# Modulation product in four column groups, attention steps respread over the units, and the values product behind the next step's scores

## The reference, cut to what matters

```
m = silu(cond) @ w_ada + b_ada            # two conditioning vectors (latent, context), 6 * 2048 columns
h = rmsnorm(x) * (1 + sc1) + sh1          # needs the first 2 * 2048 columns of m
u = h @ w_in                              # GLU input | q | k | v | gate A | gate B
att = softmax with sink over (own keys in a window of +-128, 256 cached keys) @ values
mixed = (sigmoid(gA) * conv(glu) + sigmoid(gB) * (att @ w_attn_out)) @ w_out
x = x + g1 * mixed                        # then a mixture of 16 experts and a last norm
```

## Time and profile before

| | |
|---|---|
| median of three runs | 3484.56 us |
| profiled execution | 3483.9 us, span 3482.3 us |
| PE busy | 3293.6 us (95%) |
| DVE, ACT, POOL busy | 1938.5, 1391.7, 280.5 us |
| mean granted TensorE clock | 0.975 of full |
| matmuls of `ada_unit` | 1024 in stage A, 2048 in stage S |

### The profile page before, as it was taken

One profiled execution on the slowest core, in us unless ns is written; L12 is line 12 of the kernel. 1 busy time (PEld: TensorE's weight loads), 2 busy tenths in 40 slices (PEclk: granted clock), 3 DMA queues, 4 the chain that ended last, 5 costly groups with the idle time before them and its releaser, 6 DMA issues.

```text
span 3482.3 us, 52715 instructions
## 1 busy us (share of the span) xinstructions
PE 3293.6 (95%) x20485; PEld 2765.2 (79%) x20485; DVE 1938.5 (56%) x1987; ACT 1391.7 (40%) x1669; POOL 280.5 (8%) x445
## 2 busy tenths in 40 slices
PE   7699999999989899899899999959999999999995
PEld 5499999998888888788799999946666666666663
DVE  3223332135444445454642533369998999899994
ACT  2311111122323232223331212137777777777774
POOL 0001110000010000000100111110000000000000
PEclk9899999999999999999999999979999999999997
DMA  7533332223333333333433454379999999999994
GB/s 295 202 109 127 124 117 99 81 81 139 134 136 143 133 143 131 134 141 130 168 119 118 179 163 136 99 259 364 400 376 374 391 390 371 381 391 386 374 386 146
DMA packets 124020, 745.97 MB, mean 214 GB/s; under 512 B 16720, under 2 KB 27024, under 8 KB 44096
## 3 DMA queue, kind: packets, MB, share of 16 engines
q1 hardware_dynamic: 96368, 631.28, 47.5%
q0 software_dynamic: 27504, 112.60, 10.5%
HBM read 681.60 MB, written 55.66 MB: 212 GB/s over the span
## 4 chain that ended last, share of the span: by engine, by line
PE 79%; DVE 7%; issue 5%; ACT 2%; DMA 2%; POOLq 0%; SPq 0%; POOL 0%; ACTq 0%; DVEq 0%
PE pu L813 20%; PE pu L579 15%; PE pu L580 15%; PE pu L581 15%; PE pt L563 7%; DVE elo L1603 4%; PE pt L678 2%; ACT ehi L1108 2%; PE ps L653 1%; DVE xe L1615 1%; PE pt L666 1%; PE ps L654 1%; DMA tokens_acc<-ysl,idx_all 1%; PE ps L784 1%; DMA att<-att 1%
## 5 line engine op out<-in xcount | busy, mean ns | idle before, releaser
L579 PE MATMUL pu<-hhi,whi 128*128 128x320 f32 x3328 | 1050.3, 316 | 50.1 <-DVE wlo L1185 32.1
L580 PE MATMUL pu<-hlo,whi 128*128 128x320 f32 x3328 | 1033.4, 311 | 0.0
L581 PE MATMUL pu<-hhi,wlo 128*128 128x320 f32 x3328 | 1033.2, 310 | 0.0
L1603 DVE TENSOR_TENSOR elo<-ering,ehi 128x2048 fp32r<-128x2048 f32 x384 | 874.7, 2288 | 107.0 <-ACT ehi L1108 103.8
L1108 ACT CAST ehi<-ering 128x2048 fp32r<-128x2048 f32 x384 | 731.3, 1912 | 238.3 <-PE pu L813 238.2
L579 PEld LDWEIGHTS pu<-hhi,whi 128*128 128x128 f32 x3328 | 629.9, 189 | 54.1 <-issue 43.1
L580 PEld LDWEIGHTS pu<-hlo,whi 128*128 128x128 f32 x3328 | 629.9, 189 | 2.0
L581 PEld LDWEIGHTS pu<-hhi,wlo 128*128 128x128 f32 x3328 | 629.4, 189 | 0.0
L846 ACT CAST whi<-raw 128x2048 fp32r<-128x2048 f32 x112 | 213.0, 1902 | 481.7 <-PE pu L581 463.5
L1185 DVE TENSOR_TENSOR wlo<-raw,whi 128x2048 fp32r<-128x2048 f32 x112 | 256.6, 2291 | 255.4 <-ACT whi L846 255.0
L813 PE MATMUL pu<-ehi,xhi 128*80 128x512 f32 x1024 | 322.0, 395 | 2.2
(11 more groups left out here) (264 smaller groups left out, 2854.9 us busy)
## 6 DMA issues: line engine op xcount, KB each, us to landing
ering<-in_w_experts SPq DMA_DIRECT2D x384, 1024.0 KB, 8.2
raw<-in_w_ada SPq DMA_DIRECT2D x96, 1024.0 KB, 5.0
raw<-in_w_in SPq DMA_DIRECT2D x72, 1024.0 KB, 4.9
raw<-in_w_attn_out SPq DMA_DIRECT2D x16, 1024.0 KB, 5.2
raw<-in_w_out SPq DMA_DIRECT2D x16, 1024.0 KB, 4.9
gates_tanh<-th POOLq DMA_DIRECT2D x32, 320.0 KB, 3.2
gl<-gates_tanh POOLq DMA_DIRECT2D x32, 320.0 KB, 3.4
raw<-in_w_conv_out SPq DMA_DIRECT2D x8, 1024.0 KB, 4.8
```

Of the source, the lines that this page charges most:

```text
L579: nc.tensor.matmul(o, whi[:, dk, w:w + 128], hi[:, kt, cols], start=kt == 0, stop=False)
L580: nc.tensor.matmul(o, whi[:, dk, w:w + 128], lo[:, kt, cols], start=False, stop=False)
L581: last = nc.tensor.matmul(o, wlo[:, dk, w:w + 128], hi[:, kt, cols], start=False, stop=kt == kts - 1)
L1603: nc.vector.tensor_tensor(elo[:, j % AHEAD, :], ering[:, slot, :], ehi[:, j % AHEAD, :].bitcast(F32), ALU.subtract).then_inc(ex_lo, 1)
```

## The change

1. `ada_unit` uses a stationary side of 128 x 32 (`cond32`: the two vectors and 30 columns of zeros), and the 16 k-tiles go in turn to four groups of 32 columns of the array, so to partitions 0, 32, 64 and 96 of the bank. The four partial sums are read out together (128 x 128), and a matmul with `fold` (a 128 x 2 matrix of ones and zeros made from `ident`) takes the place of the transpose: it turns the row and adds the four parts.
2. `CUT` becomes 3, 3, 3, 3, 3, 3, 2, 0 steps for the eight units. The last unit has only its `dense` and two ada units, and POOL issues `load_group` and `load_q` of the next round before it waits for that unit's gates.
3. On TensorE the scores of the next step's own keys come right behind `turn`, and the scores of its cached keys (`qk_past`) and then `pv` come behind the ada unit, or, in the third part, behind the last k-tile of `dense`. ScalarE's order follows: `turned`, read-out, `head_out`, the gate's tanh, the next step's `softmax`.
4. The attention output is read back two heads at a time into `att8`, laid over buffers of the attention stage, so that its loads wait only for the attention stores; the wait for the gates' stores comes behind them.

```
-    CUT = [NS * k // US for k in range(US + 1)]
+    CUT = [min(3 * k, NS) for k in range(US + 1)]
...
-                last = nc.tensor.matmul(bank[0:2, 0:128], cond[:, kt, :], raw[:, slot, kt * 128:kt * 128 + 128],
-                                        start=kt == 0, stop=kt == KT - 1)
+                g = 32 * (kt % 4)
+                last = nc.tensor.matmul(bank[g:g + 32, 0:128], cond32[:, kt, :], raw[:, slot, kt * 128:kt * 128 + 128],
+                                        start=kt < 4, stop=kt >= KT - 4)
             if row is not None:
-                last = nc.tensor.transpose(bank[:, 128:130], row, ident[0:2, 0:2])
+                last = row_out(bank, row)
...
+        def row_out(bank, row):
+            return nc.tensor.matmul(bank[:, 128:130], row, fold[:, :], start=True, stop=True)
...
+                if k == US - 1 and following is not None:
+                    load_group(following)
+                    load_q(following, 1)
                 pool.wait_ge(th_ready, i * US + (k + 1))
...
-        for m in range(KT):
+        for m in range(KT // 2):
             if m >= 4:
-                pool.wait_ge(attn_lo, m - 3)
-            pool.dma_start(att4[:, m % 4, :], at_d[m]).then_inc(attn_loaded[m % 4], 16)
+                pool.wait_ge(attn_lo, 2 * (m - 3))
+            pool.dma_start(att8[:, 2 * (m % 4):2 * (m % 4) + 2, :],
+                           at_d[2 * m:2 * m + 2].rearrange("h p n -> p h n")).then_inc(attn_loaded[m % 4], 16)
+        for b in range(2):
+            pool.wait_ge(th_stored[b], 16 * (SN // 2))
...
+                if k == 0:
+                    qk(i, 0)
+                    qk_past(i, 0)
+                for x in range(parts):
+                    k0, k1 = KT * x // parts, KT * (x + 1) // parts
+                    after = k1 if x < 2 else k1 - 1
+                    part(k0, after)
+                    n = steps[x] if steps else None
+                    if steps:
+                        turn(i, n)
+                        if n + 1 < NS:
+                            qk(i, n + 1)
                     if x < 2:
                         ...
+                    else:
+                        part(after, k1)
+                    if steps:
+                        if n + 1 < NS:
+                            qk_past(i, n + 1)
+                        pv(i, n)
```

More of the change, by code:

```diff
@@ L116, in build @@
     rd, o = at("rd", [128, 2], F32, o)
-    brt, o = at("brt", [16, 1], F32, o)
-    gates, o = at("gates", [128, 4], F32, o)
+    fold, o = at("fold", [128, 2], F32, o)
     row4, _ = at("row4", [128, RAW, 128], F32, X0)
     row1, _ = at("row1", [128, 128], F32, SMALL - 512)
+    cond32, _ = at("cond32", [128, KT, 32], F32, SMALL - 512 - KT * 128)
     xin, o = at("xin", [128, KT, N], F32, Y0)
@@ L381, in pool_program @@
         pool.memset(ones[:, :], 1.0 / D).then_inc(const_made, 1)
-        pool.wait_ge(const_made, 2)
+        pool.memset(cond32[:, :, :], 0.0).then_inc(const_made, 1)
+        pool.wait_ge(const_made, 3)
         pool.affine_select(out=ident[:, :], in_=ident[:, :], compare_op=ALU.not_equal, fill=1.0, base=0,
@@ L653, in qk, with qk_past @@
                 nc.tensor.matmul(ps[:, 0, 0:128 * (hi - lo)], qb, ktg[:, 128 * lo:128 * hi], start=True, stop=True)
-                last = nc.tensor.matmul(ps[:, 1, 0:PAST], qb, ktg[:, N:N + PAST], start=True, stop=True)
             else:
-                last = nc.tensor.matmul(ps[:, 0, 0:NC], qb, ktg[:, NL:N], start=True, stop=True)
-            last.then_inc(att_qk, 1)
+                nc.tensor.matmul(ps[:, 0, 0:NC], qb, ktg[:, NL:N], start=True, stop=True).then_inc(att_qk, 1)
+        def qk_past(i, n):
+            h, j = STEPS[n]
+            if j < NL // 128:
+                pe.wait_ge(att_pt, i * NS + n + 1)
+                nc.tensor.matmul(ps[:, 1, 0:PAST], qh[:, h % 2, 128 * j:128 * j + 128], ktg[:, N:N + PAST], start=True,
+                                 stop=True).then_inc(att_qk, 1)
         def turn(i, n):
@@ L686, in tensor_program, with part @@
                 steps = list(range(CUT[k], CUT[k + 1]))
[L687 to L691, removed]
+                parts = max(2, len(steps))
+                def part(k0, k1):
+                    dense(d, d, k % 2, k % 2, hhi, hlo, k0, k1, 0, KT)
+                if k == 0:
[10 more added lines that the diff above has]
+                            qk(i, n + 1)
                     if x < 2:
@@ L858, in ada_read_out @@
             act.wait_ge(raw_freed[slot], 2 * use + 2)
-            last = nc.scalar.copy(row, bank[0:2, 0:128])
+            last = nc.scalar.copy(row, bank[:, 0:128])
             if n is not None:
@@ L993, in stage_s @@
                 steps = list(range(CUT[k], CUT[k + 1]))
[L994 to L998, removed]
+                if k == 0:
+                    softmax(i, 0)
+                parts = max(2, len(steps))
+                for x in range(parts):
+                    n = steps[x] if steps else None
+                    if steps:
+                        turned(i, n)
                     if x < 2:
@@ L1001, in stage_s @@
                         ada_read_out(at_ % RAW, at_ // RAW + i * (3 * US // RAW), i * (2 * US) + (A1 + 2 * k + x - 1),
[L1002 to L1012, removed]
+                                     pt[:, 1, :], row1[:, :])
+                    if steps:
+                        head_out(i, n)
+                    if x == parts - 1:
+                        act.wait_ge(dense_mm, i * US + (QN + GN + k + 1 + CREDIT))
+                        if k >= 2:
+                            act.wait_ge(th_stored[k % 2], (i * (US // 2) + k // 2) * 16)
+                        nc.scalar.activation(th[:, k % 2, :].rearrange("p (c n) -> p c n", c=2),
+                                             pu[:, 2 * (k % 2):2 * (k % 2) + 2, 0:HALF], ACT.Tanh,
+                                             scale=0.5).then_inc(th_ready, 1)
+                        act.wait_ge(th_ready, i * US + (k + 1))
+                        act.sem_inc(psum_free[k % 2], 1)
+                    if steps and n + 1 < NS:
+                        softmax(i, n + 1)
+                    if x == parts - 1:
+                        next_unit(k)
             for b in range(2):
@@ L1194, in vector_program @@
             vec.sem_inc(used, 1)
+        vec.wait_ge(const_made, 4)
+        nc.vector.tensor_reduce(fold[:, :], ident[:, :].rearrange("p (g s) -> p s g", g=4)[:, 0:2, :], AX,
+                                ALU.add).then_inc(fold_made, 1)
         nc.vector.memset(t1[:, :], 0.0).then_inc(norm_t, 1)
@@ L1360, in stage_s @@
                 steps = list(range(CUT[k], CUT[k + 1]))
-                for x, n in enumerate(steps):
-                    maxima(i, n)
-                    normalise(i, n)
+                parts = max(1, len(steps))
+                for x in range(parts):
+                    if steps:
+                        maxima(i, steps[x])
+                        normalise(i, steps[x])
                     if x == 0 and k:
                         next_unit(k - 1)
-                    conv(i, k, x, len(steps))
+                    conv(i, k, x, parts)
             next_unit(US - 1)
```

47 lines of the change are left out of this document (24 added, 23 removed).

## The result

The changed kernel takes 3283.49 us (median; 3281.18 to 3287.09) against 3484.37 us: a ratio of 0.9426 (95% interval 0.9412 to 0.944), 201 us less. The prediction was 3332 us with a range of 3245 to 3445. The time lies in the range, and the direction was right, but the case I held likeliest, two products side by side, is not what happened.

The account below looks back on a forecast made before the run. TensorE, busy 95% of the span, was taken as the bound. From 3483.9 us, -31 (stage A) - 81 (stage S) - 25 - 6 - 10 + 1 = -152 gave 3332 us, range 3245 to 3445.

Parts of the forecast that it names:

- the case I held likeliest: Ada units: strict issue order lets only two matmuls overlap; unit 2.48 us instead of 3.74, total 3332 us, chance 0.50.
- four side by side: Rival for the ada units: a product's two instructions do not block the next group; total 3265 us, chance 0.25.
- The first sign of being wrong: Ada unit's 32 matmuls taking about 1.2 us on the timeline, meaning four at a time.
- Part 1: Ada units on column groups: stream 2.0 us against 3.38; -81 us in stage S, -31 us in stage A.
- Stage A: Loop of 28 ada units: shorter units make DMA the next bound, 2.6 us a unit; -31 us (-27 to -34).
- the +1 us for the zeroing: Before stage A: zeroing `cond32` stands ahead of POOL's first loads; estimated +1 us, from 0 to 2.
- the low clock that I named as a sign of being wrong: TensorE clock at the low level in stage A, with its lighter work between DMA waits; no size given.
- Part 2: Stage S round starts: key loads covered, TensorE then waits 2.6 us for ScalarE; 8.5 x 3 = -25 us (-20 to -33).
- Part 3: Stage S steps: covers ScalarE's copy where no ada unit runs, -6 us; chain to `pn` stays covered, 0 us.
- Part 4: Way from stage S into T: loads skip the gates' store wait, eight heads in flight; -10 us (-4 to -15).
- The slower rival: Ada units: next 32-column load no longer hides under the running matmul; 3526 us, or 3769 wholly in the open; chance 0.07.
- the one of nothing side by side: Rival for the ada units: column groups only alter where sums lie, units 0.12 us dearer; 3455 us, chance 0.10.

Follow-up runs that it names:

- the steps alone: Kernel before, with only the respread steps, next round's loads under the last unit, and values product behind the next scores: 3479.04 us, ratio 0.9984.
- The order test: Changed kernel with the same 16 products in another order over the four groups, run twice: 3376.82 us (group kt // 4) and 3288.97 us (kt // 2 % 4).
- The pairs order: Changed kernel with group kt // 2 % 4 in place of kt % 4, four matmul instructions in a row on one group: 3288.97 us (one run).
- the step drawn forward: Changed kernel with rounds written out and the next round's first scores issued inside the last unit: 3257.02 us, ratio 0.9347.
- the blocked order: Changed kernel with group kt // 4 in place of kt % 4, eight matmul instructions in a row on one group: 3376.82 us, ratio 0.9692.

## Why the prediction was right or wrong

**Right in sign and range.** The bound was read rightly: TensorE's own work in the ada units, on the path in stage S and the bound of stage A. Neither the groups alone, nor the steps alone, nor the read-back alone made the kernel slower, and the loads of the groups stay hidden. But the middle of the range is no merit of the case I held likeliest. The range covered four side by side as well, and the sum is 49 us off because two errors of opposite sign met: 77 us too slow from the groups, about 31 too fast from parts 2 to 4. The rival's 3265 us is as close as it is by the same meeting, 10 us too slow in stage S against the same 31 too fast. The first sign of being wrong that I had named, 32 matmuls in about 1.2 us, came.

**Part 1, the step that failed**, as the prediction put it: "If b must wait for a on its own group (109 ns) and later instructions may not pass it". The order test shows that they do pass, over a short distance. The stream is 0.81 us from first to last start, not 2.0, and the unit 1.33 us, not 2.48. The term of stage S was -81 and is -155 (the groups alone). The bound that I gave for four at a time, -145, missed it by 10, because it took 1.0 us for the stream, with a hand-over of 0.11 that isn't there; the changes and the row product were rightly put, at 0.48 us against 0.52. The chance of 0.25 for this case was too low; the rule of order in my argument had no row behind it.

The Trainium skill's page "TensorE: Matmul & The Clock Gate", Part 3, has matmuls start and end strictly in program order. The pairs order does not agree: four instructions on one group in a row, and still 1.12 us for 32. The Trainium skill's page "TensorEngine Tiling (Array Packing)", section Theoretical Speedup, gives up to 4x for a side of at most 32 columns; the trace agrees, 109 ns to 26. The rule of the Trainium skill's page "TensorE: Matmul & The Clock Gate", Part 3, that a weight load overlaps matmuls only where the row groups differ is not borne out either, since all four groups share the rows and 26 ns from start to start leave no room for a load of 32 columns, 110 ns in the trace, that is not overlapped.

**Stage A: mechanism and size right.** -31 was forecast, with DMA as the next bound; it is -32.5 by the experiment, at 410 GB/s. Two small things were not foreseen. The first four raw slots are freed earlier, so their reloads may share DMA with `x`; the mean over channels begins at 38.9 us where it began at 36.5. That this is the cause was not tried, but the kernel with the groups in stage S alone begins it at 35.95, with `cond32` zeroed as well, and the one with the groups alone at 39.1. So the +1 us for the zeroing, for which I had no row, cannot be seen there. The first ada unit begins 0.3 to 0.6 us later: 12.42 us before, 12.79 in the changed kernel, 12.72 with the groups alone and 13.02 with the groups in stage S alone. The 1 us for the latency of the first refill is in no run by itself. And the low clock that I named as a sign of being wrong came, without harm, as TensorE waits for DMA there.

**Part 2, the second step that failed:** "What is late next is ScalarE: at the head of a round it waits for the gates' store and reloads its table", priced at 2.6 us of waiting. The loads are covered, as said. But two links of the chain were missing. The raw unit behind the last ada unit cannot be loaded earlier, and its `whi` and `wlo` are ahead of the next maxima; and the jump back of the loop, over 3 us on TensorE and, in the chain itself, on VectorE, lay unseen under the wait for keys. With parts 2 and 3 alone the round starts cost 29 us of waiting, the first included, so the term of -25 was close to nothing. And the last unit without steps had a price that I did not foresee, 4.5 us more standstill on the way into stage T. The written-out rounds and the step drawn forward brought back 26.5 us, about what I had expected of part 2.

**Part 3: right in kind.** The copy's waits are gone (-6; part 3 was not run without part 2), and the chain from scores to `pn` stays covered in nearly all steps: of 18.7 us in ten waits, all but about 1.8 lie at the four round starts.

**Part 4: half the size.** -10 was forecast, -4.5 is measured alone. "the loads do not wait for the gates' store (about 3 us less)" failed: they are issued only 0.7 us sooner, since the attention stores are waited for as well, and the first pair takes 1.1 us longer to land than one head did. The 14.1 us of the changed kernel are not this part's doing: parts 2 and 3 alone have 14.3. In the changed kernel the gates' store (1466.93 to 1474.80) and the first pair (1467.50 to 1478.39) are under way together with units of raw weights. VectorE's splitting, which I put at 0.9 us a head, takes one every 0.76 us.

**The slower rival and the one of nothing side by side** are refuted by the 26 ns. The sum came out 49 us too slow: 74 us more from the groups in stage S and some 3 from stage A and the zeroing, against about 31 less from parts 2 to 4.

## What to carry to other kernels

A product with few stationary columns is worth spreading over the column groups of the array, the group changing from product to product; here that made its stream four times faster. The order matters: two float32 products in a row on one group cost almost nothing here, four in a row more than doubled the time, and three were not tried. When a wait is taken away, follow the chain to the next late link on every engine, and count the slot that the last use has only just freed and the jump back of the loop, on each engine. Where the wait named is for an engine, look at what that engine waited for itself. Loads that a stage needs at its start should be issued while the last unit of the stage before still runs, not at its end, where they meet the next stage's weights.

## What the runs showed of the hardware that was not expected

- Matmuls of four column groups run fully side by side, two instructions per float32 product included: 32 in 1.08 us against 3.65. With four instructions in a row on one group it is 1.12 us, with eight 2.46, and there the next group begins when three of the eight are left.
- Loads of 32 columns, 110 ns each, do not show between matmuls that start every 26 ns on average.
- The jump back over the long body of a round costs TensorE 3.1 us of standstill and VectorE 3.25; with the loops written out both are gone, and the kernel is 9.7 us faster.
- A store of 320 KB that landed after 2.4 us in the kernel before took 7.9 us beside the loads of stage T's weights in the changed one.
- TensorE at a mean granted clock of 0.73 in stage A shows no cost while DMA moves 410 GB/s; slowed by the blocked order to 2.7 us a unit, the same engine has a clock of 1.00, and stage S begins 6.7 us later.
